# Sample states four value rows to a partition, scaled by ScalarE, and head states multiplied turned round

## The reference

```python
h = x @ w_in                          # u (pooling), q, k, v, og, gates
pool_out = (window means of u - u) @ pool_w      # four groups, windows 2, 4, 8, 16
# mLSTM, 4 heads of 128, state C (value x key), normaliser n, running max m
s   = (q @ k.T) * w_intra
num = s @ v + w_inter * (C @ q)
hm  = num / max(|qn|, exp(-m_t))
C_new = decay * C + sum_s w_state[s] * outer(v[s], k[s])
n_new = decay * n + sum_s w_state[s] * k[s]
mlstm_out = sigmoid(og) * norm(hm) * g
x = layer_norm(ALPHA * x + concat(pool_out, mlstm_out) @ w_out)
```

## Time and profile before

| what | value |
|---|---|
| median of 3 runs | 668.04 us (667.41 to 669.69) |
| the profiled execution: its time, its span | 667.49 us, 665.8 us |
| PE busy | 637.3 us |
| DVE, ACT, POOL busy | 348.1, 152.0, 208.7 us |
| mean granted TensorE clock | 0.992 |

### The profile page before, as it was taken

How to read it: one execution, slowest core, us unless ns; L and a number is a source line. 1 busy time by engine, 2 the same in 40 slices (tenths; PEclk the granted TensorE clock), 3 DMA queues, 4 the chain that set the end, 5 groups by cost and what they waited for, 6 DMA issues and landing times.

```text
span 665.8 us, 8667 instructions
## 1 busy us (share of the span) xinstructions
PE 637.3 (96%) x3244; PEld 390.3 (59%) x3244; DVE 348.1 (52%) x799; ACT 152.0 (23%) x333; POOL 208.7 (31%) x245
## 2 busy tenths in 40 slices
PE   6999999999999999999999999999999999999982
PEld 3445588887787774446888774454574454333330
DVE  0283356326457792757653865355873333253445
ACT  1113221001524230002001740222324111211144
POOL 4241010100476556411101985002244342111231
PEclk9999999999999999999999999999989999999997
DMA  8994468613334345102904987454449999999698
GB/s 296 399 324 165 143 163 223 234 52 127 99 126 164 103 158 171 40 0 84 359 0 144 336 287 310 192 189 189 194 167 371 412 413 410 382 360 410 210 207 165
DMA packets 45811, 146.14 MB, mean 220 GB/s; under 512 B 5738, under 2 KB 6058, under 8 KB 41663
## 3 DMA queue, kind: packets, MB, share of 16 engines
q1 hardware_dynamic: 31559, 107.50, 42.7%
q0 software_dynamic: 12032, 33.29, 17.7%
q10 hardware_dynamic: 2176, 4.76, 2.0%
HBM read 130.34 MB, written 20.33 MB: 226 GB/s over the span
## 4 chain that ended last, share of the span: by engine, by line
PE 87%; DMA 5%; DVE 3%; ACT 1%; issue 1%; POOL 0%; ACTq 0%; DVEq 0%; POOLq 0%
PE ps L602 15%; PE ps L749 14%; PE ps L1089 12%; PE ps L511 9%; PE ps L477 8%; PE ps L1109 5%; PE ps L600 4%; DMA xn<-y_d 3%; PE ps L850 2%; PE ps L774 2%; PE ps L658 2%; PE ps L976 1%; PE ps L834 1%; PE ps L1070 1%; PE ps L673 1%; PE ps L539 1%
## 5 line engine op out<-in xcount | busy, mean ns | idle before, releaser
L749 PE MATMUL ps<-wring,P 128*128 128x512 f32 x224 | 99.2, 596 | 0.0
L749 PEld LDWEIGHTS ps<-wring,P 128*128 128x128 f32 x224 | 41.6, 190 | 49.1 <-issue 49.0
L1089 PE MATMUL ps<-wring,P 128*32 128x512 f32 (+1 forms) x288 | 65.0, 599 | 0.9 <-DVE P L2344 0.9
L1768 DVE SCALAR_TENSOR_TENSOR P<-ps,P 128x264 f32<-128x264 f32 (+1 forms) x70 | 28.8, 426 | 61.0 <-PE ps L602 44.3
L511 PE MATMUL ps<-wring,P 128*128 128x512 f32 x128 | 58.7, 617 | 1.0 <-DVE P L1723 0.8
L477 PE MATMUL ps<-xT,wring 128*128 128x312 f32 (+1 forms) x256 | 56.8, 383 | 0.0
L2505 POOL TENSOR_SCALAR rstd<-agg 128x1 f32<-128x1 f32 (+1 forms) x15 | 16.8, 1121 | 114.5 <-DVE agg L1708 114.5
L477 PEld LDWEIGHTS ps<-xT,wring 128*128 128x128 f32 x256 | 46.6, 190 | 9.3
L2344 DVE COPY P<-ps 128x512 f32<-128x512 f32 x11 | 7.6, 692 | 75.0 <-PE ps L1070 75.0
L511 PEld LDWEIGHTS ps<-wring,P 128*128 128x128 f32 x128 | 24.9, 198 | 31.6 <-issue 31.3
L1089 PEld LDWEIGHTS ps<-wring,P 128*32 128x32 f32 (+1 forms) x288 | 22.2, 130 | 36.0 <-issue 36.0
(11 more groups left out here) (444 smaller groups left out, 1103.5 us busy)
## 6 DMA issues: line engine op xcount, KB each, us to landing
wring<-in_w_in SPq DMA_DIRECT2D x5, 2048.0 KB, 9.8
wring<-in_w_gate SPq DMA_DIRECT2D x10, 1024.0 KB, 9.1
wring<-in_w_up SPq DMA_DIRECT2D x10, 1024.0 KB, 11.6
P<-in_w_down SPq DMA_DIRECT2D x10, 1024.0 KB, 11.4
P<-in_cache_mem_k SPq DMA_DIRECT2D x8, 1024.0 KB, 6.2
P<-in_cache_mem_v SPq DMA_DIRECT2D x8, 1024.0 KB, 4.9
y_d<-P POOLq DMA_DIRECT2D x1, 4160.0 KB, 32.0
wring<-in_ca_wv SPq DMA_DIRECT2D x2, 2048.0 KB, 19.6
```

The source lines that it names most:

```text
L749: last = mm(bk[:, :], src[:, k, START[t]:START[t] + TR], w[:, k, :], start=(k == 0), stop=(k == KC - 1))
L1089: last = mm(GU[p % 2][lo:lo + m, :].rearrange("p (g f) -> p g f", g=2), xgT[:, p % 3, k, lo:lo + m], gu[s][:, :, k, :], start=(k == 0), st ...
L1768: V.scalar_tensor_tensor(dst, src, scale, part, ALU.mult, ALU.add).then_inc(part_added, 1)
```

## The change

A sample's state is laid out with four value rows of one head on a partition (32 partitions to a head), in four buffers. Loads and stores are 2 KB runs. The q and k rows of a partition are those of its head alone, 256 numbers. ACT scales the state by its decay (`scale_state`) before DVE's `carried`; POOL makes an outer product into a tile of its own and adds it. Loads go in pairs, four states ahead, and reload after four updates. The sample values are turned with a stride to match, the carried part comes decayed already, and DVE's separate product with the decay goes.

A head's state is made with the weighted keys stationary and 129 value columns moving, into ring A; ACT copies it to `qT` (`take_state`), PE turns its 128x128 part later (`transpose_state`), ACT copies that (`take_turned_state`), and POOL sends it out. DVE's `take_state` goes; the statistics of `head_norm1` become `head_statistics`, run behind `products`; `head_norm2` uses `scalar_tensor_tensor`. The norm vectors' load no longer waits for the state stores, and SP waits for them before the memory loads. The diff, cut to its core (left out: declarations of semaphores and small tiles, the same number of transposes of sample values with a stride, buffer counts in the waits on stores, two plain calls):

```diff
@@ -139,8 +139,8 @@
-qk_d = dram("qk_d", [NS, 1024])
-swc_d = dram("swc_d", [NS, H])
+qk_d = dram("qk_d", [NS, H, 2 * HD])
+swc_d = dram("swc_d", [H, NS])
@@ -200,12 +200,11 @@
-BUF = (1, 0, 1, 0, 0, 1, 1, 1)
-earlier = lambda b: BUF[:b].count(BUF[b])
-Cs = [view(lo, 512, "p (h k) -> p h k", h=H) for lo in (16878, 14830)]
-qk_b = [view(lo + 512, 1024) for lo in (16878, 14830)]
-Cq_b = [x[:, 0:512].rearrange("p (h k) -> p h k", h=H) for x in qk_b]
-Ck_b = [x[:, 512:1024].rearrange("p (h k) -> p h k", h=H) for x in qk_b]
+PAIR = lambda b: b // 2 % 2
+Cs = [view(lo, 512, "p (j k) -> p j k", j=4) for lo in (14830, 15598, 16878, 17646)]
+q_rows, k_rows = [[view(lo + 512 + 128 * i, 128).unsqueeze(1) for lo in (14830, 15598, 16878, 17646)] for i in range(2)]
+qk_rows = [view(lo + 512, 256) for lo in (14830, 15598, 16878, 17646)]
+kv_outer, cq_products = view(10450, 512, "p (j k) -> p j k", j=4), view(18438, 512, "p (j k) -> p j k", j=4)
...
@@ -677,13 +678,16 @@
         pe.wait_ge(dve_free, at["keys", h])
-        bk = bank_d()
+        bk = bank_a()
         for i in range(NQT):
-            mm(bk[:, 0:HD], vn[:, i, h, 0:HD], kw[:, i, :], start=(i == 0), stop=(i == NQT - 1))
-        for i in range(NQT):
-            last = mm(bk[0:1, HD:2 * HD], vn[:, i, h, HD:HD + 1], kw[:, i, :], start=(i == 0), stop=(i == NQT - 1))
-        last.then_inc(dve_full, 1)
-        at["state", h] = nd[0]
+            last = mm(bk[:, 0:HD + 1], kw[:, i, :], vn[:, i, h, :], start=(i == 0), stop=(i == NQT - 1))
+        last.then_inc(act_full, 1)
+        at["state", h] = na[0]
+    def transpose_state(h):
+        pe.wait_ge(act_free, at["state", h])
+        nc.tensor.transpose(bank_a()[:, 0:HD], stateT[:, h, :], ident).then_inc(act_full, 1)
+        at["turned state", h] = na[0]
@@ -713,6 +717,7 @@
     transpose_heads(0)
+    transpose_state(0)
@@ -720,6 +725,7 @@
     transpose_last(1)
+    transpose_state(1)
@@ -728,6 +734,7 @@
     transpose_last(0)
+    transpose_state(2)
@@ -778,6 +785,7 @@
         mm(bk[0:TR, :], mixT[:, KC - 1, 0:TR], w[:, KC - 1, :], start=False, stop=True).then_inc(dve_full, 1)
+    transpose_state(3)
@@ -1219,6 +1227,8 @@
     sp.wait_ge(act_full, at["pool"])
+    for i in range(2):
+        sp.wait_ge(c_out[i], 64)
...
@@ -1442,6 +1452,20 @@
+    def take_state(h):
+        bk = full()
+        A(qT[:, h, 0:HD], bk[:, 0:HD], ACT.Copy)
+        A(state_n[:, h, :], bk[:, HD:HD + 1], ACT.Copy).then_inc(act_free, 1)
+    def take_turned_state(h):
+        bk = full()
+        A(stateC[:, h, :], bk[:, 0:HD], ACT.Copy).then_inc(act_free, 1)
+    def scale_state(b):
+        act.wait_ge(bounce, 64)
+        act.wait_ge(c_in[PAIR(b)], 64 * (b // 4 + 1))
+        A(Cs[b % 4], Cs[b % 4], ACT.Copy, scale=wcb[:, b:b + 1]).then_inc(c_scaled, 1)
@@ -1462,18 +1486,33 @@
     take_numerators(0)
+    take_state(0)
     weights(1)
+    scale_state(0)
+    scale_state(1)
     finish_og((0, 1))
+    scale_state(2)
+    scale_state(3)
     take_og((2, 3))
+    take_turned_state(0)
     take_numerators(1)
+    take_state(1)
     weights(2)
+    scale_state(4)
+    scale_state(5)
...
     take_projection(uT, (2, 3), 1.0, off=PADC)
+    take_turned_state(1)
     take_numerators(2)
+    take_state(2)
     weights(3)
+    scale_state(6)
+    scale_state(7)
     take_projection(uT, (0, 1), 1.0, off=PADC)
+    take_turned_state(2)
     take_numerators(3)
-    act.wait_ge(c_store[0], 16 * BUF.count(0))
+    take_state(3)
+    act.wait_ge(c_store[1], 64)
...
@@ -1857,7 +1897,7 @@
     bk = full()
-    V.tensor_copy(vsT[:, :, :], bk[:, 0:H * NS].rearrange("p (h b) -> p h b", h=H)).then_inc(dve_free, 1)
+    V.tensor_copy(vsT[:, :, :], bk[:, 0:4 * NS].rearrange("p (j b) -> p j b", j=4)).then_inc(dve_free, 1)
@@ -1903,13 +1943,6 @@
-    def take_state(h):
-        bk = full()
-        if h >= 2:
-            dve.wait_ge(c_out[h % 2], 32)
-        V.tensor_copy(Cout[:, h % 2, 0:HD], bk[:, 0:HD])
-        V.tensor_copy(Cout[0:1, h % 2, HD:2 * HD], bk[0:1, HD:2 * HD]).then_inc(dve_free, 1)
@@ -1920,7 +1953,12 @@
         link(V.reciprocal(d0, d0))
-        link(V.tensor_tensor(x[:, :, 0:HD], x[:, :, 0:HD], d0.unsqueeze(2).broadcast_to([128, NQT, HD]), ALU.mult))
+        V.tensor_tensor(x[:, :, 0:HD], x[:, :, 0:HD], d0.unsqueeze(2).broadcast_to([128, NQT, HD]), ALU.mult).then_inc(scaled_done, 1)
+    def head_statistics(h):
+        x = hn[:, h % 2]
+        dve.wait_ge(scaled_done, h + 1)
@@ -1933,7 +1971,7 @@
             x = hn[:, h % 2, t, 0:HD]
-            last = V.tensor_scalar(x, x, hagg[:, t, 0:1], den[:, 1, t:t + 1], ALU.subtract, ALU.mult)
+            last = V.scalar_tensor_tensor(x, x, hagg[:, t, 0:1], den[:, 1, t:t + 1].broadcast_to([128, HD]), ALU.subtract, ALU.mult)
@@ -1943,10 +1981,12 @@
-        dve.wait_ge(c_in[BUF[b]], 32 * (earlier(b) + 1))
-        for h in range(H):
-            last = V.tensor_tensor_reduce(out=Cq_b[BUF[b]][:, h, :], in0=Cs[BUF[b]][:, h, :], in1=Cq_b[BUF[b]][:, h, :], scale=1.0, scalar=0.0,
-                                          op0=ALU.mult, op1=ALU.add, accum_out=cq[:, h, b:b + 1])
+        dve.wait_ge(c_scaled, b + 1)
+        if b > 0:
+            dve.wait_ge(cq_done, b)
+        for j in range(4):
+            last = V.tensor_tensor_reduce(out=cq_products[:, j, :], in0=Cs[b % 4][:, j, :], in1=q_rows[b % 4][:, 0, :], scale=1.0, scalar=0.0,
+                                          op0=ALU.mult, op1=ALU.add, accum_out=cq[:, j, b:b + 1])
@@ -1972,36 +2012,37 @@
     head_norm1(0)
-    take_state(0)
     products(1)
+    head_statistics(0)
     carried(0)
+    head_norm2(0)
     carried(1)
-    head_norm2(0)
+    carried(2)
+    carried(3)
...
     head_norm1(1)
-    take_state(1)
     products(2)
-    carried(2)
-    carried(3)
+    head_statistics(1)
+    carried(4)
     head_norm2(1)
+    carried(5)
...
     head_norm1(2)
-    take_state(2)
     products(3)
+    head_statistics(2)
+    carried(6)
     head_norm2(2)
+    carried(7)
     pool_diff(2)
-    carried(4)
     pool_diff(3)
-    carried(5)
...
     head_norm1(3)
-    take_state(3)
+    head_statistics(3)
     head_norm2(3)
-    carried(6)
@@ -2032,13 +2073,11 @@
     residual(0, x1_ready)
-    carried(7)
...
     bk = full()
-    ck = P[0:NS, 10964:10964 + 512]
-    link(V.tensor_tensor(v4(ck), v4(bk[0:NS, :]), b4(sg8[:, 16:20]), ALU.mult))
-    V.tensor_tensor(vsn, vsn, ck, ALU.add).then_inc(dve_free, 1)
+    values = vsn.rearrange("b (p j) -> b p j", j=4)
+    V.tensor_tensor(values, values, bk[0:NS, :].rearrange("b (j p) -> b p j", j=4), ALU.add).then_inc(dve_free, 1)
...
@@ -2537,28 +2576,26 @@
     def state_out(h):
-        pool.wait_ge(dve_free, at["state", h])
-        pool.dma_start(o_pC[0, 0, h], Cout[:, h % 2, 0:HD]).then_inc(c_out[h % 2], 16)
-        pool.dma_start(o_pn[0, 0, h:h + 1], Cout[0:1, h % 2, HD:2 * HD]).then_inc(c_out[h % 2], 16)
-    def load_state(b):
-        i = BUF[b]
-        if earlier(b) > 0:
-            pool.wait_ge(c_store[i], 16 * earlier(b))
-        pool.dma_start(Cs[i], a["state_mlstm_C"][0, b].rearrange("h v k -> v h k")).then_inc(c_in[i], 16)
-        pool.dma_start(qk_b[i], qk_d[b].partition_broadcast(128)).then_inc(c_in[i], 16)
+        pool.wait_ge(act_free, at["turned state", h])
+        pool.dma_start(o_pC[0, 0, h], stateC[:, h, :]).then_inc(c_out[h % 2], 16)
+        pool.dma_start(o_pn[0, 0, h].rearrange("(k one) -> k one", one=1), state_n[:, h, :]).then_inc(c_out[h % 2], 16)
+    def load_states(b):
+        if b >= 4:
+            pool.wait_ge(c_store[PAIR(b)], 32)
+        for i in (b, b + 1):
+            pool.dma_start(Cs[i % 4].rearrange("p j k -> p (j k)"), a["state_mlstm_C"][0, i].rearrange("h (o j) k -> (h o) (j k)", j=4)).then_inc(c_in[PAIR(i)], 16)
+            pool.dma_start(qk_rows[i % 4], qk_d[i].unsqueeze(1).broadcast_to([H, 32, 2 * HD])).then_inc(c_in[PAIR(i)], 16)
...
         pool.wait_ge(cq_done, b + 1)
-        wv = wcb[:, b, :].unsqueeze(2).broadcast_to([128, H, HD])
-        vv = vsT[:, :, b:b + 1].broadcast_to([128, H, HD])
-        c, k = Cs[BUF[b]], Ck_b[BUF[b]]
-        G.tensor_tensor(c, c, wv, ALU.mult)
-        link(G.tensor_tensor(k, k, vv, ALU.mult))
-        G.tensor_tensor(c, c, k, ALU.add).then_inc(cupd_done, 1)
+        c = Cs[b % 4]
+        kk = k_rows[b % 4].broadcast_to([128, 4, HD])
+        link(G.tensor_tensor(kv_outer, kk, vsT[:, :, b:b + 1].broadcast_to([128, 4, HD]), ALU.mult))
+        G.tensor_tensor(c, c, kv_outer, ALU.add).then_inc(cupd_done, 1)
         pool.wait_ge(cupd_done, b + 1)
-        pool.dma_start(o_sC[0, b].rearrange("h v k -> v h k"), c).then_inc(c_store[BUF[b]], 16)
+        pool.dma_start(o_sC[0, b].rearrange("h (o j) k -> (h o) (j k)", j=4), c.rearrange("p j k -> p (j k)")).then_inc(c_store[PAIR(b)], 16)
@@ -2586,52 +2623,51 @@
     pool.wait_ge(samples_dve, STATE_READY)
-    pool.dma_start(qk_d[:, 0:512], qsn).then_inc(bounce, 16)
-    pool.dma_start(qk_d[:, 512:1024], ksn).then_inc(bounce, 16)
```

(53 more changed lines are left out.)

12 lines of the change are left out of this document (7 added, 5 removed).

## The result

The changed kernel takes 677.8 us (median of 4 runs, 677.4 to 680.7), the kernel before beside it 667.7 (4 runs): ratio 1.0154, 95% interval 1.012 to 1.0188. It is slower by 10 us; the forecast was 2.1 us faster, with a range up to 668.8 us.

What follows compares the result with a forecast made beforehand. PE was taken as the bound: head savings less transposes bring it 3.04 us sooner to the pooling products; DVE's hold leaves 2.2, the last transpose takes 0.12, so 2.1 off 668.04 gives 665.9 us, range 664.2 to 668.8.

Steps and rivals of the forecast that it cites:

- PE held once, by DVE: Pooling products: PE waits 1.0 us for DVE's third difference, then 0.2 for the fourth.
- The contention: DVE's pooling differences beside POOL's state updates: 0.8 us lost per POOL operation, five operations, 4.0 us.
- PE's work: Heads' state to projection: 4.30 us in place of 5.11, 0.81 gained for heads 0 to 2; each added transpose 0.12.
- The second rival: u projection: ACT waits for reloaded states, holding PE's fourth tile; at a 9.3 us landing PE stalls 4.2, 670.1 us; chance 0.09.
- the old start: POOL's updates of states 0 to 3 start at 185.2 us and run in a row to 198.8, before the reloads.
- the third rival: Pooling differences: contention dearer, 1.46 us per POOL operation, five cost 7.3; 1.2 us slower, 669.2; chance 0.14.
- the row that I took: Group 3's four DVE additions before: 5.26 us, 2.4 excess beside three POOL operations, giving 0.8 each.
- the steps that I had called harmless: SP's wait for state writes ahead of memory loads costs nothing; norm vectors come some 15 us sooner, while PE has other work.
- The rest is shifted as a block: Behind the pooling products: no PE wait for another 100 us, so the 2.1 us gained arrive at the end.
- the fourth rival: Behind 262 us: the gain is given back later at a transfer with its own start; near 668 us; chance 0.10.

Runs made afterwards that it cites:

- last experiment: Whole change re-ordered, against that order: POOL's update of state 6 moved behind head 2's first norm half, state 7's behind head 2's root; 0.9989 of the kernel before.
- the head part alone: Kernel before with head states multiplied turned round, copied by ACT, turned again by PE, statistics behind products; sample states as before; 1.0091 of the kernel before.
- the long hold: Kernel before with ACT copying the first pooling tile 17 times more, holding PE there; 1.0159 of the kernel before.
- three together: Kernel before with extra ACT copies ahead of each `finish_og` and six more of the first pooling tile; 676.4 us against 667.3, 1.0127.

## Why the prediction was wrong

What failed is that the sum had PE held once, by DVE, for 1.2 us, and each hold priced at its length. ACT's holds, with a chance of 0.09, cost 3.98. The contention was mis-sized, 0.8 us for a POOL operation where it was 1.14. The clock, 3.07 up to 262 and some 1.7 later, stood at nothing without a reason.

- **PE's work: right, and a little better.** 0.99 a head in place of 0.81, since the fourth score and the keys were not held as I had worked out. Transposes 0.11 each (196.67 to 196.78). The Trainium skill (TensorE: Matmul & The Clock Gate, Part 4) has about 275 ns for one in a kernel; as the duration of one record the trace agrees (0.27), as its cost it does not. Without holds PE would have been at the pooling products at 240.64; forecast 241.0.
- **The second rival came true, twice, and its sum was wrong.** I gave it 0.09, with its limit at a landing 5.1 us from issue. The first loads stood 3.6 us later than before, because POOL waited 2.29 for the landing of the decays, written turned in 4-byte pieces, and then 3.90 for their broadcast; both waits stood in the code that I had read, and the first is 0.31 in the trace of before, where that write was not turned. I kept the old start. That made the first hold, in the og projection, which the rival did not even have, and POOL began its updates at 187.40 in place of the 185.2 of the sum. For the second, the reload landed some 6.2 us after its last issue (over at 203.63, ACT released at 209.80), inside the 4.9 to 9.3 that the earlier trace rows shows and above the limit; each issue of broadcast rows took 0.72, not 0.55.
- **Contention: the mechanism right, the price too low.** 0.8 us for a POOL operation was forecast. After the change five of them (6.8 us long together), with the issues between them, lengthened DVE's work by 5.7: 1.7 on two instructions of a carried product, 3.28 on group 2, 0.72 on group 3, so 1.14 each. That is near the third rival, whose sign turned at 1.22, and near what the Trainium skill (SBUF — State Buffer, SBUF: two separate sides) says, that the one blocks the other for a whole instruction. Why the row that I took came out cheaper stays open. I put it to DVE slipping in between, but its three POOL operations stood back to back (231.63 to 236.18), and those of after have issues between them. Forecast hold 1.2, measured 2.82 idle and 3.20 by starts. With all updates out of the way it was 0.
- **The clock was missing.** I priced each hold at its length. Of the steps that I had called harmless, SP's new wait is none: SP's queue shows no wait for the state writes. For the order of the stores and the norm vectors no hold up to 262 speaks against it; no run tested them alone.
- **"The rest is shifted as a block" failed both ways.** Late arrival brought a lower clock near 500; early arrival (last experiment) was given back behind 400. A gain that is real at 262 and given back later is the fourth rival's mechanism, and its 668 is near the kernel without holds (667.0 measured); I gave it 0.10. For the changed kernel itself it could not matter, since nothing was won at 262.

**How much was clock.** The mean granted clock of the changed kernel's four runs is 0.982 to 0.985, that of before mostly 0.992 to 0.995. A mean that is lower by 0.0095 over 676 us is 12.8 us spent at the lower of the two levels (1.2 in place of 2.4 GHz), so some 6.4 us lost, by this rough count. That leaves 3.6 of the 10.0, and holds less gain, from the sum above, are 3.98 + 2.73 - 3.42 + 0.11 = 3.4. The count is an upper bound, for it also counts low clock while PE is idle: in the long hold it gives some 5 us, where 10.5 less 8.75 leaves 1.8. The profile itself has 3.07 and some 1.7 at the lower clock, 4.8.

**What stays open.** What starts the fall near 500: take the product at L924 or L932 that waits 0.49 us for ACT (465.54 before, 472.14 after). Of the nine profiles in which PE gets to it after 470 us, six have the fall between 480 and 510; of the eight in which it gets there by 467.6, two (before itself 0.91, the head part alone 0.89). Lateness favours it and does not decide it. PE is busy there; the work is small matmuls. And why PE waits longer for the cached memory values in the kernels with both parts (2.0 to 4.3 in eight profiles of ten) than in the others (0.55 to 1.4) was not tried. It matters, for in six of those eight the clock falls right behind the wait.

## To carry to other kernels

Where PE is the bound, price a stall at its length and add a range for the clock. Made holds cost here 2.6 us for 2.57, 3.4 for 2.65, 10.5 for 8.75 and, three together, 9.1 for 4.3: from nothing more to as much again. Before work is taken off PE, check the others' margin: PE comes sooner to each of their buffers, and if they are not faster the gain turns into holds. Follow a new wait back through every transfer that stands ahead of it in the issuing queue, with the landing of the new shape of transfer, not of the old one.

## What the runs showed of the hardware

- **The clock falls behind holds, not behind each.** Between 155 and 262 two holds within 4 us (0.36 and 2.46; 1.93 and 1.18; 0.76 and 2.52; 2.21 and 1.88; 0.48 and 1.89) were followed by a lower clock in every profile (eight pairs, in seven profiles), as was the one of 9.22. Single ones of 1.16 to 3.12 were in some: 1.16, 1.32, 1.70, 1.74, 1.94, 2.88 and one of 3.12 not; 1.93, 2.07, 2.57 and the other 3.12, at the same place of nearly the same kernel, yes. Later on it is the same. Of the long waits for cached memory values near 450, on a DMA and not on an engine, those of 1.96, 2.21, 2.39, 2.45, 2.62 and 3.11 were followed by a fall (0.66 to 0.73 over 5 us); those of 1.88 and 2.49 were not, though each had one of 0.7 to 0.8 some 3 us ahead of it. So a pair does not always bring it either. The two 3.12 differ in one thing more: the one with the fall had holds of 0.77 and 0.85 some 55 and 32 us ahead of it. No profile without a hold of 1.9 or more has a fall between 155 and 262. The Trainium skill (TensorE: Matmul & The Clock Gate, Part 1) says that the clock follows how busy the engine has been of late, and that what watches it runs free of the kernel; that two equal holds end differently agrees with it.
- **DVE beside POOL:** an instruction of 0.28 us with two inputs took 1.1 to 1.4 beside a POOL operation of 1.05 to 1.4, and 1.6 beside a DMA issue of POOL and the operation behind it. One of 1.12 stood beside two DMA issues of POOL and no operation (232.17 in the changed kernel).
- **Small transfers in a chain are slow:** POOL waited 2.29 us for the landing of the turned write of 8x4 decays and 3.90 for their broadcast, against 0.31 and 2.84 for the row-wise forms of before. No run changed that write alone.
